# One attention layer's tail: order of a head's softplus functions, earlier weight splits, and three smaller reorderings

## The chip, the cores and the metric

One Trainium2 chip, one core. The metric is the device time of one execution in microseconds (us). Engines are named as in the profile: PE is TensorE, ACT ScalarE, DVE VectorE, POOL GpSimd, SP the engine that issues most DMAs. PE's clock has two levels, 1.2 and 2.4 GHz; the profile gives the granted clock as a share of 2.4 GHz.

## The reference

Two transformer blocks over 512 tokens of width 1024 (batch 1): a first one (gated delta rule, pooling, a product-key expert layer), and a second one that the change is about:

```python
def second_block(...):
    h = modulate(rms_norm(x, norm_g[i, 0]), sh_m, sc_m)
    y = stick_breaking_mixer(h, sb_w_qkv[r], sb_w_o[r])
    x = x + gt_m * rms_norm(y, norm_g[i, 1])
    h = modulate(rms_norm(x, norm_g[i, 2]), sh_f, sc_f)
    y = swiglu_ffn(h, ffn_w_in[i], ffn_w_out[i])
    x = x + gt_f * rms_norm(y, norm_g[i, 3])

def stick_breaking_mixer(h, w_qkv, w_o):       # 16 heads of 64
    for q0 in range(0, s, SB_BLOCK):           # blocks of 128 queries
        z = jnp.einsum('bthd,bshd->bhts', q[:, q0:end], k[:, :end]) * scale
        sp = jnp.where(mask, jax.nn.softplus(z), 0.0)
        rest = lax.cumsum(sp, axis=3, reverse=True)
        a = jnp.exp(jnp.where(mask, z - rest, -jnp.inf))
        outs.append(jnp.einsum('bhts,bshd->bthd', a, v[:, :end]))
    return jnp.concatenate(outs, axis=1).reshape(b, s, D_MODEL) @ w_o

def swiglu_ffn(h, w_in, w_out):                # hidden width 2816
    g, u = jnp.split(h @ w_in, 2, axis=-1)
    return (jax.nn.silu(g) * u) @ w_out
```

## The kernel before, in words

The 512 tokens are four tiles of 128. Most of the time (to about 1765 us) goes to the first block and its expert layer, during which the second block of tiles 0 and 1 is woven in. What is left then, and what the change is about, is the second block of tiles 2 and 3 (256 queries, 512 keys). It runs on all engines in a hand-written order, synchronised by semaphores; each engine takes its instructions strictly in the order written.

**Projections.** `tail_values` makes the values. `tail_pair(v)` makes the queries (even v) or keys (odd v) of a pair of heads from one 512 KB weight unit; v = 0 to 3 run ahead of the head loop, v = step + 4 in steps 0 to 11 of it. SP loads the units with `pair_load(v)` into eight buffers (`pair_unit`), and with every pair of heads a small DMA (`q_swap`, L888) that brings the queries to the other half of the partitions. ACT's `pair_out` takes a pair out of PSUM.

**The head loop.** It has 17 steps on ACT, 18 on PE, one head per step. In step s PE does `scores(s)` (z of head s, semaphore `z`), then `rest(s - 1)` (the running sum of the previous head's softplus, as high and low parts and by exact matmuls with constants, semaphore `rest`), then `tail_pair(s + 4)`, then half of `values` of a pair of heads. z of even and odd heads alternate between two places in PSUM, so `scores(s)` waits for the last exponential of head s - 2 (semaphore `at`). ACT computes softplus(z) - max(z, 0) by Abs (L1951), Exp (L1961) and Ln (L1963), and the last exponential, exp(z - rest), at L1954. DVE adds max(z, 0) (L2500), rounds the sum to its high part `sp_hi` (CAST, L2504) and subtracts for the low part `sp_lo` (L2506). `rest` waits for both. `out_pair` (ACT, L926) and `out_lo` (DVE, L2493) split a finished pair of heads into `a_hi` and `a_lo`.

**Weight splits.** The output projection and both matrices of the feed-forward layer are done with each f32 number as a high and a low part at one pass each. SP loads 2 MB at a time (four units of 512 KB) into `raw[0]` or `raw[1]` (L907). ACT's `split(n)` (L1928) copies a unit to `u_hi`, POOL (L2131) or DVE (L2535) subtracts to `u_lo`. In the kernel before the first 2 MB are loaded behind all query swaps and the output of tiles 0 and 1, and units 0 to 3, whose place overlaps the projection's weight buffers, are split at the ends of ACT's steps 12 to 15. The second 2 MB overlap the queries and keys, and so wait for `scores(15)`.

**Behind the loop.** PE waits for all eight `out_lo`, then does units 0 to 3 (`split_rows`), units 4 to 7 (`split_last`), a branch with norm and residual per tile (`branch(0, t)`, ACT L1976 and L1979, DVE L2513 to L2516), transposes, `a_hi` (ACT, L2001) and `a_lo` (POOL L2127 for tile 2, DVE L2544 for tile 3), the 22 column tiles of the feed-forward input (`split_tile`), its output (`split_rows`, `split_last`), and `branch(1, t)`.

Of the kernel before, what the change touches and what calls it, by code (L numbers as in the profile page):

```python
# [389 lines left out]
def block_kernel(nc, a, out):  # L390
    ctx = ExitStack()
    with ctx:
# [238 lines left out]
        def pair_unit(v):  # L631

            n = v % WIDE
            buf = region((32, 36, 40, 44, 16, 20, 24, 28)[n], D)
            if n < 4:
                last = max(m for m in range(H_UNITS) if h_slot(m) == n)
                return buf, h_unit[n], h_turn(last) + 1 + v // WIDE
            return buf, w_unit[n], -(-(QUERY0 - n) // WIDE) + 2 + v // WIDE

        def query_swap(i):  # L640
# [136 lines left out]
        def _(sp):  # L777
# [106 lines left out]
            for i in range(AHP):  # L884
# [10 lines left out]
            for m in range(LATE):
                if m == 0:
                    sp.wait_ge(s["used"], tail_used(KD))
                    sp.wait_ge(s["seln"], T)
                elif m == 1:
                    sp.wait_ge(s["z"], AHP + AH)  # L900
                else:
                    low_pool, low_dve = group_lows(m - 2)
                    sp.wait_ge(s["u_lo"], low_pool)
                    if low_dve > 0:
                        sp.wait_ge(s["u_ld"], low_dve)
                if m < FOUT0:
                    sp.dma_start(raw[m % 2], a["w_late"][m]).then_inc(w_late[m % 2], 16)  # L907
                else:
                    rows_of = min(4, FT - 4 * (m - FOUT0))
                    sp.dma_start(rawrow[m % 2][:, 0:rows_of, :], a["w_late"][m].rearrange("p k n -> p (k n)")[:, 0:rows_of * D].rearrange("p (k n) -> p k n", n=D)).then_inc(w_late[m % 2], 16)  # L910
# [4 lines left out]

# [1708 lines left out]
```

## Time and profile before

| what | us |
|---|---|
| median of 3 runs | 2194.41 (2192.31 to 2195.76) |
| profiled execution, its own time | 2196.88 |
| span of its trace | 2195.1 |
| PE busy in the span | 1740.4 (79%) |
| DVE, ACT, POOL busy | 1332.6, 894.4, 843.1 |
| mean granted clock of PE | 0.881 of 2.4 GHz |

The busy shares are averages over stages with different limits: up to about 1765 us DMAs move over 400 GB/s, behind that the rate is 65 to 190 GB/s in most slices, and other things set the pace. In the page's chain of waits, which follows what ended last, PE has 44% of the span and DMA 24%.

### The profile page before, as it was taken

Reading aid. Unit: us, or ns where it says so; the run is one execution under the profiler, and the core shown is the slowest. Engines: PE = TensorE matmul, PEld = TensorE weight load, DVE = VectorE, ACT = ScalarE, POOL = GpSimd, SP = SyncE. Lnnn points to the kernel's source line nnn. Section 1 sums busy time; section 2 is a strip of 40 time slices with the busy share of each in tenths; the row PEclk is TensorE's granted clock in tenths of the full one; section 3 lists DMA queues with packets and bytes.
Section 4 is the critical chain, followed back from the end, with each engine's and each line's share of the span. In section 5 each row is a group of like instructions: output and inputs, shape, how many; then the busy total and the mean of one; then the engine's idle time right before and its main releaser. Section 6 shows DMA issues by size and latency. Waiting matters only on the chain.

```text
span 2195.1 us, 26077 instructions
## 1 busy us (share of the span) xinstructions
PE 1740.4 (79%) x9120; PEld 1116.8 (51%) x9120; DVE 1332.6 (61%) x2912; ACT 894.4 (41%) x2385; POOL 843.1 (38%) x679
## 2 busy tenths in 40 slices
PE   7888887756667778855877775888888799878998
PEld 6784654413324425611354421454554358757997
DVE  4686558989888766566566667656555513324442
ACT  3111344443444433445356545423223335444443
POOL 1300243457565444443344443343334300044654
PEclk9998997877788888966989887999999899978999
DMA  7266699999999999999999999999999962122443
GB/s 284 87 249 230 240 417 411 417 390 400 420 406 391 417 409 417 419 370 418 400 418 418 418 419 419 417 419 418 418 419 418 393 221 68 65 106 100 184 187 115
DMA packets 115698, 726.10 MB, mean 331 GB/s; under 512 B 13168, under 2 KB 14192, under 8 KB 44400
## 3 DMA queue, kind: packets, MB, share of 16 engines
q0 software_dynamic: 73728, 536.90, 59.7%
q1 hardware_dynamic: 41840, 187.54, 22.5%
q8 instruction: 72, 1.18, 0.2%
q14 instruction: 58, 0.48, 0.1%
HBM read 720.20 MB, written 2.10 MB: 329 GB/s over the span
## 4 chain that ended last, share of the span: by engine, by line
PE 44%; DMA 24%; DVE 16%; ACT 6%; issue 6%; POOL 4%; SPq 0%; DVEq 0%; POOLq 0%; PEldq 0%; ACTq 0%
PE ps L938 43%; DMA arena<-in_experts,arena_u 24%; DVE arena L2470 7%; POOL arena L2104 3%; ACT arena L1778 1%; DVE arena L2161 1%; ACT sel L1774 1%; DVE arena L2311 1%; ACT L1774 0%; DVE arena L2164 0%; DVE arena L2310 0%; DVE selu L2181 0%; POOL r_high L2131 0%; ACT L1622 0%; DMA middle<-in_w_late 0%
## 5 line engine op out<-in xcount | busy, mean ns | idle before, releaser
L938 PE MATMUL ps<-arena 128*128 128x256 f32 (+4 forms) x6088 | 1296.9, 516 | 378.1 <-ACT arena L1778 339.1
L938 PEld LDWEIGHTS ps<-arena 128*128 128x128 f32 (+2 forms) x6088 | 756.0, 174 | 873.1 <-ACT arena L1778 426.3
L2104 POOL DMA_INDIRECT arena<-in_experts,arena_u x512 | 587.8, 1148 | 831.3 <-PE ps L938 739.6
L2470 DVE CUSTOM_DVE_ANT_0 arena<-arena 128x1024 f32<-128x1024 f32 x512 | 649.6, 1275 | 385.1 <-DMA arena<-in_experts,arena_u 379.1
L1774 ACT ACTIVATE sel<-sel 128x1 f32<-128x1 f32 x512 | 102.9, 201 | 727.4 <-DVE sel L2470 720.1
L2131 POOL TENSOR_TENSOR r_low<-middle,r_low 128x1024 fp32r<-128x1024 f32 x48 | 122.1, 2549 | 259.8 <-ACT r_low L1928 259.8
L1778 ACT ACTIVATE arena<-arena,sel 128x32 f32<-128x32 f32 x512 | 164.5, 321 | 17.2 <-ACT sel L1774 0.3
L938 PE MATMUL ps<-r_low 128*128 128x256 f32 (+1 forms) x1104 | 140.7, 291 | 6.6 <-DVE r_low L2544 5.7
L938 PEld LDWEIGHTS ps<-r_low 128*128 128x128 f32 x1104 | 138.3, 195 | 9.0 <-issue 6.0
L1767 ACT ACTIVATE arena<-consts,arena 128x32 f32<-128x32 f32 x512 | 120.8, 308 | 0.0
L1928 ACT ACTIVATE r_low<-middle 128x1024 fp32r<-128x1024 f32 x68 | 71.6, 1056 | 75.9 <-PE ps L938 65.5
L938 PE MATMUL ps<-arena,consts 128*32 128x512 f32 (+5 forms) x672 | 91.8, 467 | 11.8 <-POOL arena L2085 4.3
L2500 DVE SCALAR_TENSOR_TENSOR upper<-ps,upper 128x896 f32<-128x896 f32 x16 | 17.5, 1092 | 126.0 <-ACT upper L1963 126.0
L2078 POOL TENSOR_TENSOR sel<-sel 128x512 f32<-128x512 f32 x32 | 42.1, 1316 | 120.1 <-DVE sel L2201 119.5
L938 PEld LDWEIGHTS ps<-arena,consts 128*32 128x32 f32 (+2 forms) x672 | 39.1, 139 | 73.9 <-issue 50.7
L938 PE MATMUL ps<-r_high 128*128 128x256 f32 (+1 forms) x232 | 52.1, 345 | 12.5 <-DVE r_high L2504 12.5
L2535 DVE TENSOR_TENSOR r_low<-middle,r_low 128x1024 fp32r<-128x1024 f32 x20 | 42.5, 2125 | 27.4 <-ACT r_low L1928 27.4
L1774 ACT ACT_TABLE_LOAD x44 | 56.5, 1283 | 0.8
L938 PE MATMUL ps<-r_low,r_high 128*128 128x512 f32 x240 | 55.0, 390 | 1.7 <-DVE r_high L2551 1.7
L2042 POOL TENSOR_TENSOR arena<-arena 128x512 f32<-128x512 f32 x28 | 37.8, 1356 | 39.6 <-DVE arena L2293 27.8
L2549 DVE TENSOR_TENSOR middle<-middle,ps 128x256 f32<-128x256 f32 x22 | 9.3, 421 | 70.1 <-ACT middle L2017 70.1
L938 PEld LDWEIGHTS ps<-r_low,r_high 128*128 128x128 f32 x240 | 44.9, 188 | 11.4 <-DVE r_high L2551 1.9
(247 smaller groups left out, 1495.2 us busy)
## 6 DMA issues: line engine op xcount, KB each, us to landing
arena<-in_w_front SPq DMA_DIRECT2D x88, 512.0 KB, 4.4
middle<-in_w_late SPq DMA_DIRECT2D x18, 2048.0 KB, 7.9
arena<-in_w_ada SPq DMA_DIRECT2D x48, 512.0 KB, 5.1
arena<-in_w_qkv SPq DMA_DIRECT2D x48, 512.0 KB, 4.7
arena<-in_w_late SPq DMA_DIRECT2D x22, 1024.0 KB, 13.7
arena<-in_w_late SPq DMA_DIRECT2D x30, 512.0 KB
arena<-in_experts,arena_u POOLq DMA_INDIRECT x512
x<-in_x SPq DMA_DIRECT2D x4, 512.0 KB, 8.7
```

What stands on the lines that cost most here:

```text
L938: return nc.tensor.matmul(out_, lhsT, rhs, start=start, stop=stop_, skip_group_check=skip)
L1767: nc.scalar.activation(gated[:, m % 2, 32 * j:32 * j + 32], fold, ACT.Copy, scale=gq[:, i % 4, 4 * q + j:4 * q + j + 1]).then_inc(s["gated ...
L1774: own.step(nc.scalar.activation(gel[:, n % 8:n % 8 + 1], dots[:, n % 8:n % 8 + 1], ACT.Gelu))
L1778: nc.scalar.activation(diag[:, m % 4, 32 * j:32 * j + 32], gated[:, m % 2, 32 * j:32 * j + 32], ACT.Copy, scale=gel[:, n % 8:n % 8 + 1]).t ...
L1928: nc.scalar.activation(u_hi[u], raw_unit(u), ACT.Copy).then_inc(s["u_hi"], 1)
L2042: tt(Bm[lv % 2][c], Am[c], m4, ALU.mult).then_inc(s["bl"], 1)
L2078: tt(onehot, onehot, fidx.rearrange("p s (o a) -> p s o a", o=1).broadcast_to([P, 2, 16, 16]), ALU.mult).then_inc(s["fpk"], 1)
L2104: nc.gpsimd.indirect_dma_start(ring[n % RING], None, a["experts"], bass.IndirectOffsetOnAxis(ap=idxq[:, i % 4, k:k + 1], axis=0),).then_in ...
L2131: nc.gpsimd.tensor_tensor(u_lo[u], raw_unit(u), u_hi[u], ALU.subtract).then_inc(s["u_lo"], 1)
L2161: ins = stt(acc[:, sh:SH], px[:, 0:SH - sh], w(CW - 1 - sh), acc[:, sh:SH], ALU.mult, ALU.add)
L2470: nc.vector.tensor_tensor_reduce(r[:, 0:D], r[:, 0:D], xrep[k % 4], 1.0, 0.0, ALU.mult, ALU.add, dots[:, n % 8:n % 8 + 1]).then_inc(s["dot ...
L2535: tt(u_lo[u], raw_unit(u), u_hi[u], ALU.subtract).then_inc(s["u_ld"], 1)
```

## The change

Five edits, all in the part behind 1765 us:

1. ACT, head loop: Exp and Ln of head s are issued right behind its Abs, ahead of the last exponential of head s - 1.
2. `split` of units 0 to 3 at ACT's steps 5, 6, 11 and 16 (`SPLIT_STEPS`), each with a wait for the projection whose weight buffer it overwrites; the load of `raw[0]` (`late_load(0)`) moves on SP to behind the second query swap. `pair_load` puts units 8 to 15 into four buffers twice (before: eight buffers once), and the loads of units 12 to 15 are issued behind swaps 3 and 4 (before: 2 and 3), each once the unit four before has been used.
3. PE starts output projection unit u once `out_lo` has done 2(u + 1) pairs, instead of all eight.
4. PE, first column tile of the feed-forward input (`first_tiles`): all products with `a_hi` of both units first, which need no `a_lo`, and the products with `a_lo` last.
5. DVE, `branch`: y times gain first, beside ACT's square root, then reciprocal, then one operation that scales and adds to x. Before: reciprocal, scale with gain, add.

```diff
         def pair_unit(v):
-            n = v % WIDE
+            n = v if v < WIDE else v % 4
             buf = region((32, 36, 40, 44, 16, 20, 24, 28)[n], D)
...
+        LOAD_BEHIND = {0: WIDE, 1: WIDE + 2, 3: WIDE + 4, 4: WIDE + 6}
+        SPLIT_STEPS = (5, 6, 11, 16)
...
             def pair_load(v):
                 if v < 4:
                     sp.wait_ge(s["slot_done"], LOADS - RING + 4 + v // 2 + 1)
-                else:
+                elif v < WIDE:
                     sp.wait_ge(s["used"], tail_used(v + 1))
+                else:
+                    sp.wait_ge(s["used"], tail_used(KD + (v - WIDE if v < WIDE + 4 else v - 4) + 1))
...
-                for v in (WIDE + 2 * i, WIDE + 2 * i + 1):
-                    if v < 2 * KD:
-                        pair_load(v)
+                if i in LOAD_BEHIND:
+                    for v in (LOAD_BEHIND[i], LOAD_BEHIND[i] + 1):
+                        pair_load(v)
+                if i == 1:
+                    late_load(0)
...
+            def first_tiles():
+                pe.wait_ge(s["a_hi"], 2)
+                for n in range(2):
+                    unit(UNIT_FIN + n)
+                    for kd in range(KD):
+                        mm(ps[:, n, 0:SH], u_hi[UNIT_FIN + n][:, kd, :], a_hi[:, kd, :], kd == 0, False, True)
+                        mm(ps[:, n, 0:SH], u_lo[UNIT_FIN + n][:, kd, :], a_hi[:, kd, :], False, False, True)
+                pe.wait_ge(s["a_lo"], 2)
+                for n in range(2):
+                    for kd in range(KD):
+                        ins = mm(ps[:, n, 0:SH], u_hi[UNIT_FIN + n][:, kd, :], a_lo[:, kd, :], False, kd == KD - 1, True)
+                    ins.then_inc(s["unit_used"], 1)
...
-            pe.wait_ge(s["o_lo"], AH // 2)
...
-            split_rows(range(UNIT_O2, UNIT_O2 + 4), o_rows, a_hi, a_lo, KD - 1)
+            for u in range(UNIT_O2, UNIT_O2 + 4):
+                pe.wait_ge(s["o_lo"], 2 * (u - UNIT_O2) + 2)
+                split_rows([u], o_rows, a_hi, a_lo, KD - 1)
...
+                if u < UNIT_O2 + 4:
+                    sc.wait_ge(s["used"], tail_used(KD + (6, 8, 14, 16)[u]))
...
                     nc.scalar.activation(sp, z_of(h), ACT.Abs).then_inc(s["lnp"], 1)
+                    sc.wait_ge(s["lnp"], 3 * AHP + 3 * h + 1)
+                    nc.scalar.activation(sp, sp, ACT.Exp, scale=-1.0).then_inc(s["lnp"], 1)
+                    sc.wait_ge(s["lnp"], 3 * AHP + 3 * h + 2)
+                    nc.scalar.activation(sp, sp, ACT.Ln, bias=1.0).then_inc(s["lnp"], 1)
                 if done >= 0:
                     sc.wait_ge(s["rest"], AHP + done + 1)
                     nc.scalar.activation(spb[done % SPS], z_of(done), ACT.Exp).then_inc(s["at"], 1)
...
-                if h < AH:
-                    ... (the same Exp and Ln, behind out_pair and pair_out)
-                if 12 <= step < 16:
-                    split(UNIT_O2 + step - 12)
+                if step in SPLIT_STEPS:
+                    split(SPLIT_STEPS.index(step))
...
             def branch(k, t):
+                ve.wait_ge(s["ysq"], H_SQ + 2 * (2 * k + t) + 1)
+                own.step(tt(dst, y, gtrow[:, k, :], ALU.mult))
                 ve.wait_ge(s["ysq"], H_SQ + 2 * (2 * k + t + 1))
                 own.step(nc.vector.reciprocal(stat[:, 3, t:t + 1], stat[:, 3, t:t + 1]))
-                own.step(stt(dst, y, stat[:, 3, t:t + 1], gtrow[:, k, :], ALU.mult, ALU.mult))
-                tt(x[:, 2 + t, :], x[:, 2 + t, :], dst, ALU.add).then_inc(...)
+                stt(x[:, 2 + t, :], dst, stat[:, 3, t:t + 1], x[:, 2 + t, :], ALU.mult, ALU.add).then_inc(...)
```

The place on ACT where the head loop's steps 12 and 13 meet, before. L1951 is Abs, L1961 and L1963 are Exp and Ln of the same head, L1954 the last exponential of the head before, L926, L1885 and L1886 take results out of PSUM, L1928 is a split:

```order
L1951 ACTIVATE upper<-ps 128x896 [waits z,av]
L1954 ACTIVATE upper<-ps 128x896 [waits rest]
L926 ACTIVATE r_low<-ps 128x256 [waits av]
L1885 ACTIVATE arena<-ps 128x256 [waits used]
L1886 ACTIVATE arena<-ps 128x256
L1961 ACTIVATE upper<-upper 128x896 [waits lnp]
L1963 ACTIVATE upper<-upper 128x896 [waits lnp]
L1928 ACTIVATE r_low<-middle 128x1024 [waits w_late0]
L1951 ACTIVATE upper<-ps 128x896 [waits z,av]
L1954 ACTIVATE upper<-ps 128x896 [waits rest]
```

The same place in the changed kernel, where Abs is L1980, Exp and Ln L1982 and L1984, the last exponential L1987 and the copies L936, L1912 and L1913:

```order
L1980 ACTIVATE upper<-ps 128x896 [waits z,av]
L1982 ACTIVATE upper<-upper 128x896 [waits lnp]
L1984 ACTIVATE upper<-upper 128x896 [waits lnp]
L1987 ACTIVATE upper<-ps 128x896 [waits rest]
L936 ACTIVATE r_low<-ps 128x256 [waits av]
L1912 ACTIVATE arena<-ps 128x256 [waits used]
L1913 ACTIVATE arena<-ps 128x256
L1980 ACTIVATE upper<-ps 128x896 [waits z,av]
L1982 ACTIVATE upper<-upper 128x896 [waits lnp]
L1984 ACTIVATE upper<-upper 128x896 [waits lnp]
```

Exp and Ln now stand ahead of the last exponential and of the copies, and no split stands between the two steps.

PE at the start of the feed-forward input, before. `arena,x` is the last transposes, `r_low 128x256` the products of the column tiles (24 per unit):

```order
L938 MATMUL ps<-arena,x 128x128 x7
L938 MATMUL ps<-r_low 128x256 [waits a_lo,u_lo]
L938 MATMUL ps<-r_low 128x256 x23
L938 MATMUL ps<-r_low 128x256 [waits u_lo]
L938 MATMUL ps<-r_low 128x256 x23
```

And in the changed kernel:

```order
L948 MATMUL ps<-arena,x 128x128 x7
L948 MATMUL ps<-r_low 128x256 [waits u_lo,a_hi]
L948 MATMUL ps<-r_low 128x256 x15
L948 MATMUL ps<-r_low 128x256 [waits u_lo]
L948 MATMUL ps<-r_low 128x256 x15
L948 MATMUL ps<-r_low 128x256 [waits a_lo]
L948 MATMUL ps<-r_low 128x256 x15
```

32 of the 48 matmuls now stand ahead of the wait for `a_lo`.

SP behind the projection loads of the first pairs in the changed kernel. L911 is a query swap, L894 a projection load, L881 the 2 MB load of `raw[0]`, which stood behind the last swap and the output before:

```order
L894 DMA arena<-in_w_qkv 128x1024 [waits used] x2
L881 DMA middle<-in_w_late 128x4096 [waits seln,used]
L911 DMA arena<-arena 64x256 [waits qkv]
L911 DMA arena<-arena 64x256
L911 DMA arena<-arena 64x256 [waits qkv]
L911 DMA arena<-arena 64x256
L894 DMA arena<-in_w_qkv 128x1024 [waits used] x2
```

The 2 MB load now stands ahead of six of the eight query swaps and ahead of the loads of units 12 to 15.

## Rows read from the trace of the kernel before

**Rows 1.** Busy time by stretch: us, then busy (and count) of each engine, PE clock:

```profile
1812.00:1903.57 91.57, 91.57 (x593) 74.85 (x592) 31.39 (x39) 46.53 (x61) 0.00 (x0) 1.00 0.14 44
1903.57:1955.00 51.43, 31.52 (x170) 25.27 (x168) 18.56 (x16) 19.27 (x25) 9.37 (x4) 0.70 0.36 132
1996.20:2127.50 131.30, 129.56 (x1056) 129.39 (x1056) 59.80 (x81) 53.00 (x67) 73.92 (x29) 0.98 0.46 175
```

**Rows 2.** Waits of PE, 1812 to 1996: total us, times, longest:

```profile
PE ps L938 <- DVE r_high L2504: 12.5, 4, 5.7
```

**Rows 3.** Timeline, step 8: start, us, what, count [idle before <-releaser]:

```profile
1871.36 1.13 PE L938 MATMUL ps<-arena 64*128 64x256 f32 x8
...
1872.90 0.92 ACT L1951 ACTIVATE upper<-ps 128x896 f32<-128x896 f32 x1 [2.95 <-PE ps L938]
...
1875.16 0.92 ACT L1954 ACTIVATE upper<-ps 128x896 f32<-128x896 f32 x1 [1.34 <-PE ps L938]
...
1879.52 1.13 PE L938 MATMUL ps<-arena 64*128 64x256 f32 x8
```

**Rows 4.** Timeline, head 0, from Abs to its last exponential:

```profile
1812.42 0.92 ACT L1951 ACTIVATE upper<-ps 128x896 f32<-128x896 f32 x1 [0.71 <-PE ps L938]
...
1815.33 1.09 DVE L2500 SCALAR_TENSOR_TENSOR upper<-ps,upper 128x896 f32<-128x896 f32 x1 [40.84 <-ACT upper L1963]
1816.46 0.56 DVE L2504 CAST r_high<-upper 128x768 fp32r<-128x768 f32 x1
...
1819.69 0.92 ACT L1954 ACTIVATE upper<-ps 128x896 f32<-128x896 f32 x1 [1.53 <-PE ps L938]
```

**Rows 5.** Timeline, steps 12 and 13:

```profile
1903.57 1.13 PE L938 MATMUL ps<-arena 64*128 64x256 f32 x8
...
1907.37 0.92 ACT L1954 ACTIVATE upper<-ps 128x896 f32<-128x896 f32 x1 [1.33 <-PE ps L938]
...
1908.34 1.08 PE L938 MATMUL ps<-upper,arena 128*64 128x256 f32 x8 [1.01 <-ACT upper L1954]
...
1909.35 1.13 PE L938 MATMUL ps<-arena 64*128 64x256 f32 x8
...
1920.17 1.06 ACT L1928 ACTIVATE r_low<-middle 128x1024 fp32r<-128x1024 f32 x1 [9.24 <-DMA middle<-in_w_late]
```

**Rows 6.** Chain that ended last, 1911 to 1996: start, us, what:

```profile
1911.18 8.97 DMA middle<-in_w_late
...
1925.82 2.63 DVE r_high L2504
...
1928.49 4.65 PE ps L938 x20
...
1954.99 0.93 ACT upper L1954
...
1960.57 9.49 POOL r_high L2131 x4
...
1970.11 5.77 PE ps L938 x24
...
1977.04 0.21 ACT stat L1979
...
1993.21 2.89 DVE r_low L2544
```

**Rows 7.** Busy time by stretch, as Rows 1, where PE's clock falls:

```profile
1914.00:1916.00 2.00, 2.00 (x11) 2.00 (x11) 0.00 (x0) 0.00 (x0) 0.00 (x0) 0.50 0.92 344
```

**Rows 8.** DMA issues: KB each, median us from issue to landing:

```profile
middle<-in_w_late SPq DMA_DIRECT2D x18, 2048.0 KB, 7.9
arena<-in_w_qkv SPq DMA_DIRECT2D x48, 512.0 KB, 4.7
```

**Rows 9.** Timeline, PE at units 0 to 3 and at the feed-forward input's start:

```profile
1958.63 11.17 PE L938 MATMUL ps<-r_low 128*128 128x512 f32 x48 [0.94 <-DVE r_low L2493]
...
1996.23 14.01 PE L938 MATMUL ps<-r_low 128*128 128x256 f32 x93 [5.69 <-DVE r_low L2544]
```

More of the change, by code:

```diff
@@ L636, in pair_unit @@
                 last = max(m for m in range(H_UNITS) if h_slot(m) == n)
-                return buf, h_unit[n], h_turn(last) + 1 + v // WIDE
-            return buf, w_unit[n], -(-(QUERY0 - n) // WIDE) + 2 + v // WIDE
+                return buf, h_unit[n], h_turn(last) + 1 + max(0, v // 4 - 1)
+            return buf, w_unit[n], -(-(QUERY0 - n) // WIDE) + 2
         def query_swap(i):
@@ L864, in _, with late_load @@
                 half_unit(H_FF + j)
+            def late_load(m):
+                if m == 0:
+                    sp.wait_ge(s["used"], tail_used(KD))
+                    sp.wait_ge(s["seln"], T)
+                elif m == 1:
+                    sp.wait_ge(s["z"], AHP + AH)
+                else:
+                    low_pool, low_dve = group_lows(m - 2)
+                    sp.wait_ge(s["u_lo"], low_pool)
+                    if low_dve > 0:
+                        sp.wait_ge(s["u_ld"], low_dve)
+                if m < FOUT0:
+                    sp.dma_start(raw[m % 2], a["w_late"][m]).then_inc(w_late[m % 2], 16)
+                else:
+                    rows_of = min(4, FT - 4 * (m - FOUT0))
+                    sp.dma_start(rawrow[m % 2][:, 0:rows_of, :], a["w_late"][m].rearrange("p k n -> p (k n)")[:, 0:rows_of * D].rearrange("p (k n) -> p k n", n=D)).then_inc(w_late[m % 2], 16)
             def pair_load(v):
@@ L868, in pair_load @@
                     sp.wait_ge(s["slot_done"], LOADS - RING + 4 + v // 2 + 1)
+                elif v < WIDE:
+                    sp.wait_ge(s["used"], tail_used(v + 1))
                 else:
-                    sp.wait_ge(s["used"], tail_used(v + 1))
+                    sp.wait_ge(s["used"], tail_used(KD + (v - WIDE if v < WIDE + 4 else v - 4) + 1))
                 sp.dma_start(buf, a["w_qkv"][v // 2 + KD * (v % 2)]).then_inc(landed, 16)
@@ L894, in _ @@
                 sp.dma_start(out.rearrange("b (t p) d -> p (b t) d", p=P)[:, t, :], x[:, t, :]).then_inc(s["out"], 16)
[L895 to L900, printed above, removed]
-                else:
[L902 to L910, printed above, removed]
+            for m in range(1, LATE):
+                late_load(m)
             for t in range(2, T):
@@ L1444, in split_tile @@
                 for kd in range(KD):
-                    if u == UNIT_FIN and kd == 0:
-                        pe.wait_ge(s["a_lo"], 2)
                     mm(out_, u_hi[u][:, kd, :], rows_hi[:, kd, :], kd == 0, False)
@@ L1592, in _ @@
                     pe.wait_ge(s["ffd"], FT + j - 3)
+                if j == 0:
+                    first_tiles()
+                    continue
                 for n in range(2):
@@ L1958, in _ @@
                     pair_out(step // 2 + 1)
-                if h < AH:
-                    sc.wait_ge(s["lnp"], 3 * AHP + 3 * h + 1)
-                    nc.scalar.activation(sp, sp, ACT.Exp, scale=-1.0).then_inc(s["lnp"], 1)
-                    sc.wait_ge(s["lnp"], 3 * AHP + 3 * h + 2)
-                    nc.scalar.activation(sp, sp, ACT.Ln, bias=1.0).then_inc(s["lnp"], 1)
-                if 12 <= step < 16:
-                    split(UNIT_O2 + step - 12)
+                if step in SPLIT_STEPS:
+                    split(SPLIT_STEPS.index(step))
             out_pair(sc, AHP - 1)
```

4 lines of the change are left out of this document (2 added, 2 removed).

## The prediction

> **What bounds the kernel now.** I read the busy time by stretch first. From 1812 us, where the head loop starts, to 1903.57, where step 12's `scores` start, PE is busy all 91.57 us at a granted clock of 1.00; from there to 1955, the end of the last head, it is busy 31.52 of 51.43 us at a mean clock of 0.70 [rows 1]. The first stretch belongs to PE: the projections of steps 0 to 11 fill every gap. The second belongs to a chain through ACT and DVE. The waits of PE name it: 12.5 us in 4 waits on the CAST that makes `sp_hi` [rows 2].
>
> The timeline then gives one step of each kind. Step 8, with a projection, takes 8.16 us, 1871.36 to 1879.52 [rows 3]; its last exponential, at 1875.16, has long been done when PE needs it. In steps 12 and 13 there is no projection [rows 5], and ACT meets the first split, which waits 9.24 us for its load: nothing of step 13 starts before 1920.17. The load is issued at 1911.18 and takes 8.97 us [rows 6]. The chain adds two more costs: a CAST of 2.63 us, against 0.56 us for the same CAST in head 0 [rows 4, 6], and a `rest` of 4.65 us at PE's lower clock, against 2.67 us (1816.46 + 0.56 to 1819.69) [rows 4, 6]. Behind the loop the chain goes over POOL's four lows to 1970.06 and over the late `a_lo` to 1996.23 [rows 6, 9]; then PE is full again, 129.56 of 131.30 us [rows 1].
>
> **Steps 0 to 11: nothing.** The new ACT order brings the softplus of head s forward and makes the last exponential of head s - 1 later: Abs, Exp and Ln take ACT about 2.8 us (DVE starts 2.91 us after Abs starts, 1812.42 to 1815.33, less a hand-over of some 0.1) [rows 4], where the exponential used to start 2.26 us after Abs (1872.90, 1875.16) [rows 3]. So it is 0.5 us later; PE needs it for `values`, which stands between the projection and the next `scores` at 1879.52, over 3 us after 1875.16. The CAST ends 4.60 us after Abs (1812.42 to 1817.02) [rows 4]; `rest` wants it when the next step's `scores` are over, 6.62 + 1.13 us after Abs [rows 3], so 3 us of cover.
>
> The splits at steps 5, 6 and 11 put POOL's subtraction beside DVE. It can start after Abs + 2.8 + 0.9 + 1.06, that is 4.8 us, when the CAST (to 4.60) is over; only the subtraction for `sp_lo` can meet it. Bounds for each: 0, or 2.07 (2.63 - 0.56) as in steps 13 to 15; I take 0, because of the 3 us of cover, and keep 3 x 2.07 = 6.2 us for a rival.
>
> The Trainium skill (SBUF — State Buffer, "SBUF: two separate sides") calls the port pair of DVE and GpSimd an exclusive lock that whichever operation starts first holds to its end, and counts DVE operations with two SBUF inputs in. By that rule `sp_lo`'s subtraction, begun first, would make POOL wait and lose nothing itself; begun second it would lose up to POOL's whole operation, 2.4 us. The trace agrees for the CAST (2.63 beside POOL) and shows no `sp_lo` subtraction beside POOL. This speaks against steps 5 and 11 only by the price that the rival above already has.
>
> **Steps 12 to 16.** I lay the changed loop from step 12's `scores` at 1903.57, the same time in both. In a step without projection:
> - `scores` start to Abs start: 1.54 us [rows 3].
> - Abs to the previous head's last exponential: the later of ACT's 2.8 us and the end of `rest`, 3.80 us behind the `scores` start (1871.36 to 1875.16) [rows 3]. ACT is later: 1.54 + 2.8 = 4.34 us from the `scores` start.
> - exponential to the next `scores`: in an even step `values` waits for it and comes between, 1.98 us (1907.37 to 1909.35); in an odd step `scores` itself waits, 0.97 us (1907.37 to 1908.34) [rows 5].
>
> So even steps take 6.32 us, odd ones 5.31 us: `scores` at 1909.89 (13), 1915.20 (14), 1921.52 (15). The last head has nothing behind it: 1.54 us to Abs and 7.27 us from Abs to its last exponential (1812.42 to 1819.69) [rows 3, 4] give 1930.33. In the profile of before this is 1954.99 [rows 6]. Gain: 24.66 us. The split waits, the blocked CASTs and the low clock are all in that difference. It assumes clock 1.00: PE's longest idle gap here is about 1.7 us, between the end of `rest(11)` and `values`.
>
> **The loads.** `raw[0]` is issued behind swap 1 (about 1814) and is wanted in step 5, over 30 us later; it takes 7.9 us [rows 8]. The second 2 MB wait for `scores(15)`: issue at 1923.0, landed by 1930.9 (7.9 us) or 1932.0 (8.97 us) [rows 6, 8]; POOL starts 5.58 us behind the last exponential and one split of 1.06 us stands ahead of it [rows 5, 6], so ACT wants them 4.5 us behind, at 1934.8. Covered. Projection unit 12 can load once unit 9 is used, in step 5 (about 1854), needs 4.7 us [rows 8], and is read in step 8 at about 1875 [rows 3].
>
> **Output projection.** PE starts units 0 to 3 about 0.95 us sooner behind the last exponential, since the wait for the last `out_lo` moves to unit 3; they take 11.17 us [rows 9]. But units 4 to 7 wait for POOL: its four lows start 5.58 us and end 15.1 us behind the last exponential (1954.99, 1960.57, 1970.06) [rows 6], and ACT's table load and splits ahead of them are unchanged. I cost this edit at 0; the cover that eats it is POOL.
>
> **Branches.** The gain product runs beside ACT's square root; what leaves the path is the root, 0.21 us [rows 6], since reciprocal and two 1024-wide operations stay. Two branches lie on the path for certain: 0.4 us (bounds 0 and 0.8).
>
> **First column tile.** PE now starts when `a_hi` of tile 3 is done, when DVE starts `a_lo` (1993.21), instead of 1996.23 [rows 6, 9]: 3.0 us. The 32 matmuls without `a_lo` are 4.8 us at the 0.15 us each of 93 in 14.01 us [rows 9], so `a_lo` (2.89 us) is hidden. Bounds: 0, if the splits for column tile 2, which wait for units 8 and 9 to be used, become what PE waits for; 4.3, if PE, started sooner, also gets its clock back sooner. I take 3.0; nothing behind can absorb it, because PE is full to 2127 [rows 1].
>
> **Sum.** 24.66 + 0.4 + 3.0 = 28.1 us. The profiled execution's own time was 2196.88 (span 2195.1 and 1.8 around it); it becomes 2168.8. The median of the runs is 2.5 us below the profiled one, so 2194.41 - 28.1 = 2166.3.
>
> **Rivals.**
> - *The clock falls in steps 12 to 16.* For: before, it fell in this stretch, after waits of 1.01 us [rows 5] and of up to 5.7 us [rows 2], and then stood at 0.50 while PE was full [rows 7]. Against: it is 1.00 through the same kernel's full stretch, and the new loop has PE busy for about 20 of 27 us. Price, with `rest` at 4.65 for 2.67 and everything else of PE doubled: steps 13 and 14 take 8.0 and 9.9 us, the last head 13.3 us: 31.2 for 20.4, so up to 10.7 us, to 2177; one short fall costs 2 to 4 us.
> - *Splits inside the full steps block DVE*: 6.2 us, 2172.5. For: CASTs of 2.63. Against: the cover above.
> - *The late steps don't shorten*, because something not seen holds them at 8.05 us: last exponential at 1903.57 + 3 x 8.05 + 8.81 = 1936.5, 6.2 us later, 2172.5.
> - *The wait moves to the second load.* If 2 MB took 13 us rather than 8 to 9, 1936 instead of 1934.8: 1.2 us, 2167.5.
> - *Slower: the projection weights starve PE.* Four buffers instead of eight for units 8 to 15, and units 12 to 15 issued a swap later. If they land behind their turn, PE idles in steps 8 to 11, and its clock halves: 8.05 us more for each of 4 steps, 32 us, net 4 slower, 2198. It decides once the landing takes more than 16 us longer than 4.7 us. Against: that is the slack, 1859 to 1875, and DMA is busy only 0.14 of that stretch [rows 1].
> - *No effect*: the stall is only moved, 2194.
>
> **How the numbers follow.** Chances: forecast 0.66, clock 0.13, blocked DVE 0.06, long steps 0.05, second load 0.05, no effect 0.02, slower 0.03. The forecast's own range is 2163 to 2169 (branches and first tile at their bounds, 0.5 for the steps). To hold 8 in 10 the range must take in most of the clock rival and both at 2172.5: 2162.5 to 2176. Faster by over 0.2% (4.4 us, what a measurement here can tell from none): 0.95; within: 0.02; slower: 0.03.
>
> **What would show it.** Right: no ACT wait on `middle<-in_w_late` in the loop; the last exponential some 26.8 us behind step 12's `scores`; CASTs of 0.56 us; PE clock near 1.00 from 1903 to 1934; PE starting the column tiles before DVE's `a_lo` ends; PE waiting about 1.2 us for POOL before unit 4. Wrong: PE idle before step 12, a clock of 0.50 inside the loop, an ACT wait on the second 2 MB, or odd and even late steps above 6.5 us.

## The result and the profile after

The median went from 2193.36 us (4 runs, 2190.89 to 2195.76) to 2166.94 us (4 runs, 2160.32 to 2168.82): ratio 0.9875, interval 0.9855 to 0.9896. The forecast was 2166.3.

The profiled execution took 2160.32 us, span 2158.5. Its head loop began at 1804.18 us, 8.24 us sooner than in the profile of before [rows 4]. That is no gain of the change: over the profiles below it began anywhere from 1804.18 to 1818.24 (at 1814.31 in e1, the same kernel again), behind a stage that no experiment edits. So I compare stretches counted from the loop's first Abs, not spans.

Busy time by stretch, kernel after: the full steps, steps 12 to the last exponential, from there to the first column tile, and 131 us behind it. Columns as in rows 1.

```profile
1804.18:1895.34 91.16, 91.16 (x592) 74.47 (x590) 32.65 (x40) 49.35 (x64) 7.14 (x3) 1.00 0.20 67
1895.34:1922.08 26.74, 21.20 (x170) 17.12 (x168) 11.11 (x14) 15.59 (x21) 1.40 (x1) 1.00 0.34 123
1922.08:1959.85 37.77, 28.77 (x144) 23.25 (x144) 9.76 (x21) 21.97 (x36) 21.53 (x10) 0.94 0.30 112
1959.85:2091.20 131.35, 129.63 (x1057) 129.42 (x1057) 62.86 (x82) 54.22 (x68) 75.81 (x30) 0.98 0.48 177
```

The first stretch is as long as before (1812.42 to 1903.57 is 91.15 us [rows 4, 5]) and PE fills it at clock 1.00. The second is 26.74 us where it was 51.42 (1903.57 to 1954.99 [rows 5, 6]), and the clock is 1.00 where it was 0.70 [rows 1]. The third is 37.77 us where it was 41.24 (1954.99 to 1996.23 [rows 6, 9]); there the clock isn't full, 0.94. The last is full of PE work in both.

Timeline of the kernel after, steps 12 to 16: start, us, what, in brackets the idle time before.

```profile
1895.34 1.13 PE L948 MATMUL ps<-arena 64*128 64x256 f32 x8
...
1900.61 1.08 PE L948 MATMUL ps<-upper,arena 128*64 128x256 f32 x8 [1.52 <-ACT upper L1987]
...
1901.63 1.13 PE L948 MATMUL ps<-arena 64*128 64x256 f32 x8
...
1907.00 1.10 PE L948 MATMUL ps<-arena 64*128 64x256 f32 x8 [0.81 <-ACT upper L1987]
...
1913.27 1.13 PE L948 MATMUL ps<-arena 64*128 64x256 f32 x8
...
1918.85 0.56 DVE L2532 CAST r_high<-upper 128x768 fp32r<-128x768 f32 x1
...
1922.08 0.92 ACT L1987 ACTIVATE upper<-ps 128x896 f32<-128x896 f32 x1 [3.59 <-PE ps L948]
```

The steps take 6.29, 5.37 and 6.27 us, the last head 8.81. The CAST is 0.56 us, where it was 2.63 in rows 6, and ACT meets no load. PE's longest single wait in these steps is 1.6 us.

Waits of PE in the same kernel, 1805 to 1975 us: total, times, longest. The wait on the CAST, 12.5 us in rows 2, is 1.6.

```profile
PE ps L948 <- ACT upper L1987: 4.9, 4, 1.5
...
PE ps L948 <- DVE r_high L2532: 1.6, 1, 1.6
PE ps L948 <- POOL r_high L2159: 1.3, 1, 1.3
```

The splits now stand in full steps. Step 5, timeline: POOL starts its subtraction behind DVE's CAST and meets DVE's `sp_lo` subtraction. The last line is PE's `rest`, which reads the CAST's result.

```profile
1844.13 1.05 ACT L1957 ACTIVATE r_low<-middle 128x1024 fp32r<-128x1024 f32 x1
1844.59 0.56 DVE L2532 CAST r_high<-upper 128x768 fp32r<-128x768 f32 x1
1845.18 0.96 DVE L2534 TENSOR_TENSOR r_high<-upper,r_high 128x768 fp32r<-128x768 f32 x1
1845.26 3.09 POOL L2159 TENSOR_TENSOR r_low<-middle,r_low 128x1024 fp32r<-128x1024 f32 x1 [100.11 <-ACT r_low L1957]
...
1848.07 0.74 PE L948 MATMUL ps<-r_high 128*128 128x256 f32 x4
```

The CAST is over at 1845.15, POOL starts at 1845.26, 0.11 us later. But `rest` begins only at 1848.07, 2.92 us behind the CAST's end, so by these rows a CAST held up by POOL (2.63 us in rows 6, 2.07 more) would still have been in time.

Behind the loop, chain of waits of the kernel after:

```profile
1926.53 1.07 ACT r_high L1957
...
1927.66 9.46 POOL r_high L2159 x4
1937.17 5.75 PE ps L948 x24
1942.94 1.12 ACT arena L2004 x2
1944.09 1.24 DVE arena L2542
```

POOL's four lows start 5.58 us behind the last exponential, as before (5.58 [rows 6]), and the chain goes over them again. What moved is the start of the first column tile, which no longer waits for `a_lo`:

```profile
1959.83 3.10 DVE L2573 TENSOR_TENSOR r_low<-upper,r_low 128x1024 fp32r<-128x1024 f32 x1 [1.25 <-ACT r_low L2029]
...
1959.85 6.35 PE L948 MATMUL ps<-r_low 128*128 128x256 f32 x29 [2.68 <-ACT r_low L2029]
```

In rows 6 and 9 PE started 3.02 us behind `a_lo`'s start; here the two start together.

From first Abs to the last instruction the tail took 379.59 us before and 351.30 after: 28.29 less, of it 24.67 up to the last exponential, 3.47 from there to the first column tile, 0.15 behind it.

### The profile page after: what moved, and what is told of

It reads as the page before. It is cut to its first block, busy times and chain, and to the rows that moved or that the text cites. A ratio compares the mean times of both kernels' runs of the same rounds, so it can differ in the third digit from the quotient of the medians.

```text
span 2158.5 us, 26088 instructions
## 1 busy us (share of the span) xinstructions
PE 1718.6 (80%) x9120; PEld 1103.6 (51%) x9120; DVE 1325.5 (61%) x2912; ACT 893.7 (41%) x2385; POOL 852.4 (39%) x679
## 4 chain that ended last, share of the span: by engine, by line
PE 44%; DMA 24%; DVE 15%; ACT 7%; issue 6%; POOL 4%; DVEq 0%; SPq 0%; POOLq 0%; ACTq 0%; PEldq 0%
PE ps L948 43%; DMA arena<-in_experts,arena_u 24%; DVE arena L2498 7%; POOL arena L2132 3%; ACT arena L1805 1%; DVE arena L2189 1%; ACT sel L1801 1%; ACT L1801 1%; DVE arena L2339 1%; DVE arena L2192 0%; POOL r_high L2159 0%; ACT L1649 0%; DVE arena L2338 0%; DVE selu L2220 0%; DVE selu L2209 0%
## 5 line engine op out<-in xcount | busy, mean ns | idle before, releaser
L2132 POOL DMA_INDIRECT arena<-in_experts,arena_u x512 | 593.9, 1160 | 819.7 <-PE ps L948 728.0
L948 PE MATMUL ps<-arena,consts 128*32 128x512 f32 (+5 forms) x672 | 90.7, 465 | 12.5 <-POOL arena L2113 4.9
L948 PE MATMUL ps<-r_high 128*128 128x256 f32 (+1 forms) x232 | 46.2, 318 | 1.6 <-DVE r_high L2532 1.6
```

What stands on the lines that cost most here:

```text
L948: return nc.tensor.matmul(out_, lhsT, rhs, start=start, stop=stop_, skip_group_check=skip)
L2132: nc.gpsimd.indirect_dma_start(ring[n % RING], None, a["experts"], bass.IndirectOffsetOnAxis(ap=idxq[:, i % 4, k:k + 1], axis=0),).then_in ...
```

## The experiments

All edits are against the kernel after, which is rebuilt in the first. "Loop" is first Abs to last exponential, "to tile" from there to the first column tile, "tail" first Abs to the end, all from the profiled execution.

| kernel | loop | to tile | tail | ratio to before |
|---|---|---|---|---|
| before | 142.57 | 41.24 | 379.59 | |
| after | 117.90 | 37.77 | 351.30 | 0.9875 |
| e1 after again | 117.91 | 38.80 | 352.03 | 0.9875 (0.9857 to 0.9894) |
| e3 old splits and loads | 130.55 | 38.16 | 363.85 | 0.9934 (0.9915 to 0.9954) |
| e4 early load, splits at 12 to 15 | 117.91 | 37.12 | 349.44 | 0.9878 (0.9857 to 0.99) |
| e2, e5 old order | 132.26 | 38.80 | 366.66 | 0.9951, 0.9946 (0.993 to 0.9963) |
| e6 no `first_tiles` | 117.91 | 40.96 | 353.41 | 0.987 (0.984 to 0.99) |
| e7 one wait for `out_lo` | 117.91 | 37.14 | 349.47 | one run |
| e8 lows of units 4 to 7 on DVE | 117.90 | 36.82 | 349.08 | 0.9874 (0.985 to 0.9897) |
| e9 old order, splits at 12 to 15, early load | 139.18 | 38.82 | 373.44 | 0.9986 (0.9969 to 1.0002) |
| e10 old order, filler matmuls | 128.94 | 37.59 | 361.28 | 0.9946 (0.9928 to 0.9964) |
| e11 combined | 116.89 | 37.23 | 349.53 | 0.9866 (0.9849 to 0.9884) |
| e12 old branches | 117.92 | 38.39 | 351.67 | one run |

Every kernel with ACT's new order and the early load has the same loop to 0.02 us (e11 apart, which changes it). "To tile" and "tail" move more between kernels with equal work there: after, e1 and e4 differ by up to 1.7 and 2.6 us. Times of whole runs move by more still. Small edits are therefore read from the loop or from single rows.

**e1: the kernel after once more.**

> The changed kernel once more, unchanged, in five rounds. Theory: the whole gain is made behind 1765 us, 28.3 us from the first Abs of the head loop to the last DVE operation (379.6 us before), and what the runs of one kernel differ by (8 us between two profiles) is made ahead of the loop. So the stretch from the first Abs to the last residual add comes out at 351.3 us, within 0.5, whatever the run's own time, and the median over five rounds is 28 us below before. Rival: the edits also move the part ahead of the loop, the median gain then stays clear of 28 us and the first Abs starts more than 2 us sooner or later than before in the median.

Measured 2167.83 us (2165.53 to 2171.63) against 2194.97; loop 117.91. The tail, 352.03, is 0.73 from the first profile, just over the 0.5 I had allowed: 1.03 of that arises between the last exponential and the tile. Busy time over that stretch: PE has the same 144 matmuls at a clock of 0.90 where the first profile had 0.94, and e7, with the same loop, had 1.00.

```profile
1932.22:1971.02 38.80, 29.79 (x144) 24.27 (x144) 9.76 (x21) 21.97 (x36) 22.56 (x10) 0.90 0.29 109
```

```profile
1923.72:1960.86 37.14, 28.17 (x144) 22.65 (x144) 9.75 (x21) 21.97 (x36) 20.82 (x9) 1.00 0.30 114
```

These 1.66 us arise in one place, the transposes of tile 3. They start 32.36 and 32.43 us behind the last exponential, each time behind a PE wait of 3.51 us, and take 3.76 us in e1, 2.02 in e7:

```profile
1964.58 3.76 PE L948 MATMUL ps<-arena,x 128*128 128x128 f32 x16 [3.51 <-DVE arena L2550]
```

```profile
1956.16 2.02 PE L948 MATMUL ps<-arena,x 128*128 128x128 f32 x16 [3.51 <-DVE arena L2549]
```

The other kernels lie between (e4 2.02, after 2.73, e3 and e12 3.1, e5 and e6 3.75). The wait ahead is the same in all of them; why the clock falls behind it in some and not in others isn't shown.

**e2 and e5: edit 1 undone.** Exp and Ln stand behind the last exponential again; the new splits stay.

```diff
                     nc.scalar.activation(sp, z_of(h), ACT.Abs)...
-                    ... activation(sp, sp, ACT.Exp, scale=-1.0); activation(sp, sp, ACT.Ln, bias=1.0)
                 if done >= 0:
                     nc.scalar.activation(spb[done % SPS], z_of(done), ACT.Exp)...
...
+                if h < AH:
+                    ... activation(sp, sp, ACT.Exp, scale=-1.0); activation(sp, sp, ACT.Ln, bias=1.0)
```

> The changed kernel with edit 1 undone: ACT's order of before, splits at steps 5, 6, 11 and 16. Chain theory, from the rows of before: from step 12's scores, steps of 5.8, 6.9 and 8.1 us and 12.5 us for the last head, 33.4 us to the last exponential, where the changed kernel takes 26.7: stretch from the first Abs to the end 351.3 + 6.7 = 358.0 us. If PE's clock falls because PE idles more, up to 8 us more. Rival (the order is worth nothing, all the gain is the lost stall): 351.3 us.

Five runs of e2 lie at 2177.53 to 2186.84 us, ratio 0.9951 (0.9927 to 0.9975). The sixth, the profiled one, took 4903.06 us, for a reason that wasn't found, and can't give the stretches; so the kernel was profiled again as e5:

> The same kernel as e2 (edit 1 undone), whose profile fell on a disturbed execution, while its timed runs came 16 us above the changed kernel instead of the 6.7 us of the chain at full clock. Theory now: with ACT's old order PE idles longer between its pieces (about 15 of 33 us), its clock falls to 0.50 in steps 13 to 16, and the low clock lengthens the chain's own matmuls: first Abs to last exponential 117.9 + 14 to 17 us = 132 to 135 us, granted clock well under 1.00 from step 12 to the last exponential. Rival (the order alone, clock full): 124.6 us, and the rest of the 16 us somewhere else in the trace.

2185.99 us, ratio 0.9946; loop 132.26, and 14.4 us more than after, where the first expectation had 6 to 7. It lies within the 132 to 135 of the second, but by luck: that one put everything above the 6 to 7 down to the clock, and the rows give the clock 3.3 us and caught CASTs, which it didn't have, 4.4. Timeline of e5 in a full step: the CAST is caught behind POOL's subtraction and takes 2.63 us, and PE waits for it although it has a projection.

```profile
1870.72 2.35 POOL L2160 TENSOR_TENSOR r_low<-middle,r_low 128x1024 fp32r<-128x1024 f32 x1 [7.67 <-ACT r_low L1957]
1870.85 2.63 DVE L2533 CAST r_high<-upper 128x768 fp32r<-128x768 f32 x1
...
1871.56 0.38 PE L948 MATMUL ps<-r_high 128*128 128x256 f32 x1
...
1873.54 0.62 PE L948 MATMUL ps<-r_high 128*128 128x256 f32 x3 [1.60 <-DVE r_high L2533]
```

In the kernel after, the same POOL subtraction starts after the CAST (rows of step 5 above), because the softplus was ahead. Under the old order there is hardly any cover either: at 0.56 us this CAST would have ended at 1871.41, and PE came to want it at about 1871.94, when the first matmul of `rest` was over: some 0.5 us, where a caught CAST loses 2.07. CASTs are caught in steps 5 and 6, which costs 3.13 us before step 12 starts; the third, of head 11, is caught just ahead of step 12's `scores`, and PE waits for it in step 12. From step 12's scores to the last exponential it takes 37.97 us. The clock falls twice; busy time by stretch of the two steps where it did, with its mean of 0.79 in each:

```profile
1919.56:1927.86 8.30, 6.36 (x40) 5.08 (x38) 2.94 (x4) 3.49 (x5) 0.00 (x0) 0.79 0.39 142
...
1935.90:1950.50 14.60, 9.46 (x59) 8.08 (x57) 5.55 (x7) 4.62 (x7) 0.00 (x0) 0.79 0.39 145
```

**e10: how much of that is the clock.** The old order as in e5, and three matmuls whose result nobody reads on PE in each of steps 13 to 16, where it waits for the CAST.

```diff
+                if step >= 13 and step <= AH:
+                    for _ in range(3):
+                        mm(ps[:, 4, 0:SH], const(C_ONES), v2[2][:, 0:SH])
```

> The kernel of e5 (old ACT order, new splits) with three extra 128x256 f32 matmuls of 0.43 us each on PE in steps 13 to 16, ahead of the rest that waits for DVE, into a PSUM bank that nobody reads; they only keep PE busy in its waits. Theory: the clock is a cost of its own in e5 (0.87 over the late steps, 0.50 in the last rest). With it held at 1.00 the last exponential comes 4 to 5 us sooner although PE has 5 us more work: first Abs to last exponential 127 to 129 us for 132.3. Rival (the clock doesn't matter): 132.3 or longer.

Busy time of e10 from step 12's scores to the last exponential:

```profile
1910.54:1945.19 34.65, 27.65 (x194) 21.41 (x192) 14.44 (x16) 15.44 (x21) 1.96 (x1) 1.00 0.26 95
```

The clock is 1.00 throughout and the loop 128.94 us, within the 127 to 129 expected. The difference from e5 in this stretch, 37.97 - 34.65 = 3.32 us, is what the clock cost, at least, since the filler matmuls take PE time too. I had expected 4 to 5. The rest, 34.65 - 26.74 = 7.91 us, is the order itself, 1.26 of it in step 12 (7.03 us against 5.77 in e9), which meets the third caught CAST. The 14.36 us between e5 and after are so 3.1 by the CASTs caught ahead of step 12, 1.3 by the third, 6.7 by the order, 3.3 by the clock. The timed ratio, 0.9946, is that of e5: timing can't show 3.3 us (the interval is 8 us wide), the profile does.

**e3: edit 2 undone.** Splits and loads as before (`pair_unit` and `pair_load` too, left out below), order new.

```diff
-        SPLIT_STEPS = (5, 6, 11, 16)
+        SPLIT_STEPS = (12, 13, 14, 15)
...
-                if i == 1:
-                    late_load(0)
...
-            for m in range(1, LATE):
+            for m in range(LATE):
```

> The changed kernel with edit 2 undone: loads and splits of units 0 to 3 as before (load behind all query swaps, splits at steps 12 to 15), the new ACT order kept. Chain theory: ACT waits for the load until 17 us behind step 12's scores; then steps of 10 to 12 us with the clock low, last exponential 41 to 44 us behind step 12's scores: stretch 366 to 369 us. Rival (the split's wait was covered by the order too): under 356 us.

2180.35 us (2178.02 to 2181.71), tail 363.85 us, 2 less than the lower end: the stall in step 13 is as expected, but step 14 and the last head take 8.56 and 8.81 us and not 10 to 12 each, because the clock comes back (1.00 in the last head). Timeline of e3: ACT is held by the load in step 13, PE stands still for 11.16 us, and its next matmuls run at half speed.

```profile
1917.72 1.06 ACT L1947 ACTIVATE r_low<-middle 128x1024 fp32r<-128x1024 f32 x1 [11.19 <-DMA middle<-in_w_late]
...
1922.49 2.04 PE L938 MATMUL ps<-arena 64*128 64x256 f32 x8 [11.16 <-ACT upper L1977]
1922.70 0.56 DVE L2522 CAST r_high<-upper 128x768 fp32r<-128x768 f32 x1
1923.37 3.10 POOL L2149 TENSOR_TENSOR r_low<-middle,r_low 128x1024 fp32r<-128x1024 f32 x1 [2.16 <-ACT r_low L1947]
```

But no CAST is caught, although all four splits stand in the late steps: with the new order the CAST is over before POOL starts.

**e4: which half of edit 2.** The early load stays, the splits go back to steps 12 to 15.

```diff
-        SPLIT_STEPS = (5, 6, 11, 16)
+        SPLIT_STEPS = (12, 13, 14, 15)
```

> The changed kernel with the splits of units 0 to 3 at steps 12, 13, 14 and 15 again, but the load still early (behind swap 1). Theory: what counted was the landing, not the step. In the new order a split stands behind the last exponential, POOL's subtraction falls between DVE's CASTs, and nothing is lost: stretch 351.3 us, within 0.5. Rival: splits in the short steps stand in the way on ACT (1.06 us each) and block the CAST (2.07 us each): 354 to 360 us.

2167.52 us, ratio 0.9878; loop 117.91, the same as after. With the new order, the whole of edit 2's gain in the loop is the load's; which steps the splits stand in makes no difference.

**e9: the other combination.** e4's splits with the old order.

> The changed kernel with ACT's old order and the splits back at steps 12 to 15; only the load stays early. Theory: the landing stall (10.2 us of step 13's start) goes, but each of the four splits is again issued right behind Ln, so POOL starts just ahead of DVE's CAST and blocks it, in step 12 now too: first Abs to last exponential 142.6 - 10.2 + 2.1 = 134.5 us (131 to 137 with the clock), four CASTs of 2.6 us. Rival (landing is all that counted): 118 to 125 us.

2192.19 us, ratio 0.9986: no difference from before that can be told; loop 139.18, 4.7 over what I expected and 2.2 over the upper end. Timeline of e9: DVE, each time POOL has just started.

```profile
1912.80 2.62 DVE L2533 CAST r_high<-upper 128x768 fp32r<-128x768 f32 x1
1923.37 2.62 DVE L2533 CAST r_high<-upper 128x768 fp32r<-128x768 f32 x1
1934.88 2.63 DVE L2533 CAST r_high<-upper 128x768 fp32r<-128x768 f32 x1
1944.97 2.62 DVE L2533 CAST r_high<-upper 128x768 fp32r<-128x768 f32 x1
```

The clock is lost as well, and costs more than the upper end had allowed for it: 0.68 in the last two stretches, and the last head takes 18.72 us.

```profile
1920.53:1933.59 13.06, 7.95 (x38) 6.03 (x38) 4.67 (x3) 6.24 (x8) 2.34 (x1) 0.68 0.00 0
1933.59:1952.31 18.72, 11.96 (x59) 9.66 (x57) 9.68 (x7) 5.65 (x7) 4.68 (x2) 0.68 0.52 193
```

The load's wait is gone here and almost nothing comes of it: 3.4 us of the loop. Under the old order caught CASTs and the clock take its place; how the time divides between the two wasn't separated here.

**e6: edit 4 undone.** The first column tile with `split_tile` and its wait for `a_lo`.

```diff
+                    if u == UNIT_FIN and kd == 0:
+                        pe.wait_ge(s["a_lo"], 2)
...
-                if j == 0:
-                    first_tiles()
-                    continue
```

> The changed kernel with edit 4 undone: the first column tile waits for both halves of a_lo again. Theory: PE starts it 3.0 to 3.3 us later behind the last exponential (37.1 to 38.8 us in three traces, so 40 to 42), and the stretch from the first Abs is 3 us longer (354.3), of which nothing is absorbed. Rival (column tile 2's splits set the pace): start later, end the same, under 0.5 us.

To tile 40.96 us, so 2.2 to 3.8 more than the five other kernels with this loop and POOL's lows (37.12 to 38.80); against e1 it is 2.16, against after 3.19. The tail is 353.41, where 354.3 was expected. The rows of e6: `a_lo` took 2.04 us, not the 2.89 of rows 6.

```profile
1974.06 2.04 DVE L2572 TENSOR_TENSOR r_low<-upper,r_low 128x1024 fp32r<-128x1024 f32 x1 [1.26 <-ACT r_low L2028]
...
1976.24 3.97 PE L948 MATMUL ps<-r_low 128*128 128x256 f32 x17 [4.85 <-DVE r_low L2572]
```

It was shorter because POOL was within 0.95 us of its end when `a_lo` began. e6 has the slow transposes (3.75 us), so the fair comparison is from `a_lo`'s start: to the tile it is 2.18 us in e6 and 0.02 in after, 2.16 for edit 4; the rest of the 3.19 is the clock in the transposes. 2170.8 us, ratio 0.987: timing can't tell it from after.

**e7: edit 3 undone.**

```diff
-            for u in range(UNIT_O2, UNIT_O2 + 4):
-                pe.wait_ge(s["o_lo"], 2 * (u - UNIT_O2) + 2)
-                split_rows([u], o_rows, a_hi, a_lo, KD - 1)
+            pe.wait_ge(s["o_lo"], AH // 2)
+            split_rows(range(UNIT_O2, UNIT_O2 + 4), o_rows, a_hi, a_lo, KD - 1)
```

> The changed kernel with edit 3 undone: one wait for all eight out_lo. Theory: POOL's lows of units 4 to 7 set the pace, so units 0 to 3 start 3.64 us instead of 2.63 us behind the last exponential and unit 4 still at 15.1 us; first Abs to unit 4 unchanged at 133.0 us. Rival: the wait was worth its 1.0 us.

One run, 2160.17 us. Units 0 to 3 start 3.64 us behind the last exponential instead of 2.63, unit 4 at 15.11 instead of 15.09: the microsecond is eaten by POOL, as worked out.

**e8: POOL's share of the lows.** Units 4 to 7 have their low parts made by DVE.

```diff
-            return n >= UNIT_FIN + 4 and n % 3 == 0
+            return 4 <= n < UNIT_FIN or n >= UNIT_FIN + 4 and n % 3 == 0
```

> The changed kernel with the low parts of units 4 to 7 made by DVE (1.22 us each when POOL is still) instead of POOL (2.37 us each). Theory: POOL's chain is all that keeps unit 4 at 15.1 us behind the last exponential; with DVE done by about 11 us, PE goes straight on from unit 3 and unit 4 starts at 13.8 us, the stretch from the first Abs 1.2 us shorter (350.1 and less). Rival: DVE waits for the split on ACT or shares its port with POOL, and unit 4 stays at 15 us or later.

Timeline of e8: DVE makes the four in 4.63 us where POOL took 9.45, and PE goes on at once, 13.64 us behind the last exponential.

```profile
1933.21 4.63 DVE L2564 TENSOR_TENSOR r_high<-middle,r_high 128x1024 fp32r<-128x1024 f32 x4 [1.95 <-ACT r_high L1957]
...
1941.31 4.92 PE L948 MATMUL ps<-r_high,r_low 128*128 128x512 f32 x21
```

So edit 3's cover was POOL: without it unit 4 starts 1.45 us sooner and the transposes of tile 3 1.58 us sooner (30.78 for 32.36 us behind the last exponential). The bound is then PE's own 11 us for units 0 to 3. Timed 2167.73, ratio 0.9874: not to be told from after.

**e11: e8, and Ln behind the last exponential in steps 12 and 14.** In even steps `values` waits for the last exponential, which ACT's Ln delays.

```diff
-                    sc.wait_ge(s["lnp"], 3 * AHP + 3 * h + 2)
-                    nc.scalar.activation(sp, sp, ACT.Ln, bias=1.0).then_inc(s["lnp"], 1)
+                    if h not in (12, 14):
+                        sc.wait_ge(s["lnp"], 3 * AHP + 3 * h + 2)
+                        nc.scalar.activation(sp, sp, ACT.Ln, bias=1.0).then_inc(s["lnp"], 1)
```

> e8's kernel (low parts of units 4 to 7 on DVE), and in steps 12 and 14 ACT issues Ln behind the last exponential of the head before instead of ahead of it, since in these two steps rest is done 0.5 us before Ln is. Theory: 0.5 us less in each of the two steps, first Abs to last exponential 116.9 for 117.9 us; unit 4 at 13.6 us; the stretch to the end near 348.5 us. Rival: the later Ln makes the CAST late by as much, 117.9 us or more.

Loop 116.89 us as expected: steps 12 and 14 take 5.77 and 5.76 us instead of 6.29 and 6.27. The tail, 349.53, is 1.0 over what I expected and above e8's 349.08, although the loop is shorter: the transposes take 3.76 us here, 3.36 in e8. Against e1, with the same 3.76, "to tile" is 1.57 us shorter. 2166.73 us (2164.67 to 2169.6), ratio 0.9866 (0.9849 to 0.9884). It has the lowest ratio of all, but after's 0.9875 lies in its interval; two microseconds in 2167 aren't shown by timing.

**e12: edit 5 undone.**

```diff
-                own.step(tt(dst, y, gtrow[:, k, :], ALU.mult))
...
-                stt(x[:, 2 + t, :], dst, stat[:, 3, t:t + 1], x[:, 2 + t, :], ALU.mult, ALU.add)
+                own.step(stt(dst, y, stat[:, 3, t:t + 1], gtrow[:, k, :], ALU.mult, ALU.mult))
+                tt(x[:, 2 + t, :], x[:, 2 + t, :], dst, ALU.add)
```

> The changed kernel with edit 5 undone. Theory: from the start of a branch's Square to its x 4.1 us instead of 3.9 (the square root of 0.2 us is back on the path), 0.25 us in each of two branches on the path, 0.5 us in all. Rival: nothing, the three DVE operations cost as much in either order.

Timelines, e12 and then the kernel after, from ACT's sum of squares to its next one:

```profile
1953.32 0.19 ACT L2004 ACTIVATION_READ_ACCUMULATOR arena<-ps 128x1 f32 x1
...
1956.56 1.06 ACT L2012 ACTIVATE arena<-x 128x1024 f32<-128x1024 f32 x1 [2.81 <-DVE x L2544]
```

```profile
1943.86 0.19 ACT L2004 ACTIVATION_READ_ACCUMULATOR arena<-ps 128x1 f32 x1
...
1946.86 1.06 ACT L2012 ACTIVATE arena<-x 128x1024 f32<-128x1024 f32 x1 [2.58 <-DVE x L2545]
```

3.24 against 3.00 us: 0.24 us for this branch, 0.25 expected, and 0.24 for the last branch of all (4.12 against 3.88 us from its Square to the end). Of the two branches ahead of the first column tile only one counts: the Square of tile 3 starts 26.4 us behind the last exponential in both kernels.

## Why the prediction was right

Right as a whole, and by the mechanism it named: the tail shortened by 28.29 us (27.56 in e1) against a sum of 28.1. That the median lies only 0.6 us from the forecast is partly luck. Against before in the same series of runs it fell by 26.42 us (27.14 in e1), 1.7 less than the sum, and before itself came out 1.05 us lower than the 2194.41 I started from; the interval allows 22.8 to 31.8 us. A slip in the working: branches and first tile at their bounds and 0.5 us for the steps give 2164.1 to 2170.2 for the forecast's own range, not 2163 to 2169.

- *Steps 12 to 16, -24.66 us.* Measured -24.67. The laid-out step times were 6.32, 5.31, 6.32 and 8.81; measured 6.29, 5.37, 6.27 and 8.81. Both kinds of step hold: the last exponential starts 4.32 us (step 12) and 4.33 us (step 13) behind the `scores`, straight behind ACT's Ln, for the 4.34 worked out, and then comes `values` or `scores`. e11 takes Ln out of the way in the even steps and gets 0.52 us a step; the odd ones were not tested so. "The late steps don't shorten" is refuted.
- *The split waits, the blocked CASTs and the low clock are all in that difference.* True, and they don't add. The loop is 142.57 us with both edits undone, 130.55 with the order alone, 132.26 with the splits alone, 117.90 with both: 12.0 and 10.3 alone, 24.7 together, 2.3 of it by their meeting. The early load without the order gives only 3.4 (e9) and with it 12.65 (e4).
- *The clock.* It stayed at 1.00 in the loop, in all the profiled kernels with the new order and the early load, so the rival of up to 10.7 us didn't come. It was near: under the old order, with the same work, it fell in two of four stretches (e5) and cost 3.3 us, and three filler matmuls a step held it (e10). I had 0.13 on this rival; nothing here says that the margin is large.
- *Splits inside the full steps: 0.* Right, and the reason stands: 3 us of cover were worked out, and `rest` begins 2.92 us behind the CAST's end in step 5 (3.07 in step 6), more than the 2.07 that a caught CAST loses. It wasn't even needed, since the CAST ended before POOL started, by 0.11 us. The rival comes true under the old order, where the cover is some 0.5 us in step 6 of e5: there PE waits 1.60 us, and the three caught CASTs cost 3.13 + 1.26 = 4.4 us, for the 6.2 I gave the rival.
- *`sp_lo`'s subtraction beside POOL.* In step 5 DVE's ran at its usual 0.96 us and POOL's took 3.09 us, against 2.35 in step 6, where it didn't meet one (3.10 in step 11, where it did). POOL lost 0.74 us, a little less than the 0.88 that was left of DVE's 0.96 when it started. The Trainium skill (SBUF — State Buffer, "SBUF: two separate sides") calls the port pair of DVE and GpSimd an exclusive lock held by whichever began first, DVE's operations with two SBUF inputs included; the trace agrees, with these numbers.
- *The loads.* The second 2 MB load was issued at 1914.74 and ACT's split at 1926.53 didn't wait. The third made ACT wait 4.4 us at unit 8, which the prediction didn't have; PE, busy with units 0 to 7, wasn't held by it.
- *Output projection, 0.* Right, and by the reason given: e7 leaves unit 4 where it was, e8 removes POOL and gains 1.45 us there. PE's wait for POOL was 1.28 us, 1.2 forecast.
- *Branches, -0.4.* One branch measured 0.24, and one of them lies ahead of the first column tile (e12), the other at the very end: 0.48 us for the two. The whole can't be seen in the tail.
- *First column tile, -3.0.* Right in these two profiles (3.02 by rows 6 and 9), but 2.16 in e6, since `a_lo` itself takes 1.5 to 3.3 us over these profiles, by how much of POOL's work it meets; so the size is that of this pair of profiles. The rest of the 3.47 us between the last exponential and the tile is the transposes of tile 3: they start 0.28 us sooner (32.64 and 32.36 us behind the last exponential), 0.24 of that by the branch (e12), and take 2.73 us for 2.91, by the clock.
- *No step of the projections starved*: PE was busy 91.16 of 91.16 us before step 12. The slower rival is refuted.

Open: "to tile" differs by 1.7 us between equal kernels because PE's clock falls in the transposes of tile 3 or doesn't; what decides that isn't shown, and no run changed it there by itself. Why the loop's start moves by 14 us between profiles wasn't looked into.

## What to carry to other kernels

Where a stretch is held by a chain of dependent steps, lay out one period of the changed chain engine by engine from single rows; that gave each step here to 0.06 us. Work out the cover against the event that ends it, and in the order that will run: the same splits cost nothing with ACT's new order and 4.4 us with its old one. Then undo each edit on its own with the others kept: two edits of 10 and 12 us gave 24.7 together, and the load alone 3.4, because a wait that goes uncovers the next. And read small edits from rows, since the whole run's time can't tell 2 us.

## What the runs showed of the hardware

- A DVE CAST of 0.56 us takes 2.62 to 2.64 us when POOL's subtraction of 2.35 started 0.13 us before it, every time (e5; 0.13 to 0.14 in e9), and a POOL subtraction that starts 0.08 us behind DVE's two-input subtraction takes 3.09 instead of 2.35, DVE's keeping its 0.96. In these rows the one that starts second pays.
- In e5 PE's clock fell to 0.50 behind waits of 0.99, 1.01 and 1.91 us, came back, stayed at 1.00 over waits of 2.04, 1.01 and 1.36 us, and was at 0.50 again behind one of 3.74. In the kernel after, with waits of 0.81 to 1.6 us and PE busy 21.20 of 26.74 us, it stayed at 1.00. In e10 it was busy 27.65 of 34.65 us and stayed at 1.00 too, with one wait of 2.25 us.
- Behind one and the same PE wait of 3.51 us, the 16 transposes of tile 3 took 3.76 us in e1 and 2.02 in e7, and values between in other kernels with the same work: the longest wait alone doesn't tell whether the clock falls.
